# Order of the block products in a seven-product projection, the short convolution of the second strip in halves, and the place of one load wait

## The chip, the cores and the metric

The kernel runs on one core of one Trainium2 chip. The metric is the device time of one execution in microseconds (us), lower is better. Three runs of the kernel before gave 2369.01, 2370.47 and 2370.71 us, median 2370.47 us. All data are float32.

## What is computed

One hybrid decoder layer on 1024 tokens of width 1024. The change touches the input projection and what stands directly behind it:

```
y    = rmsnorm(x, norm_mix_g)
proj = y @ w_in                      # columns: u 512, v 512, q|k|v 1536, z 512, a 4, b 4
u, v, qkv, z, a, bb = split(proj)
out_a = gmlp_chunk_mixer(gelu(u), rmsnorm(gelu(v), gm_norm_g), gm_ws, gm_bs)
qkv  = silu(causal_dwconv(qkv, conv_w))          # 4 taps over the tokens, per channel
q, k = l2norm(q), l2norm(k)                      # per head of 128 channels
out_b = rmsnorm(gated_delta_rule(q, k, v, g, beta), dn_norm_g) * silu(z)
h    = x + concat(out_a, out_b) @ w_out
h    = h + moe_ffn(rmsnorm(h))       # top 4 of 32 experts, clamped SwiGLU
out  = rmsnorm(h, final_norm_g)
```

The factors `dn_norm_g` of the output norm are folded into silu(z) here.

## The kernel before

The program is three blocks with a barrier of all engines between them: projections, mixers (gMLP gate, delta rule, output projection, router) and the expert FFN. The change lies in the first block. Every engine runs its own list in program order and meets the others only at semaphores; DMAs are issued by SyncE in the order of its list.

**First half of the block: tokens by tiles (t = 0 to 7, 128 tokens each).** For tile t + 1 ScalarE sums the squares of x (`x_square`), VectorE scales them to a mean, GpSimd takes the inverse root (`x_root`, which calls `rsqrt`, L225), VectorE scales x (L583), TensorE transposes it (L456), VectorE writes it to `yT` with the norm's gain (L589). TensorE multiplies tile t with the u, v, z, a and b columns of `w_in` in four pieces n = 0 to 3 of 384 or 392 columns (L491); the transposes of tile t + 1 stand between pieces 1 and 2. At t = 0 piece 2 also waits until VectorE has copied the transposed parameters (L572 to L574, semaphore `par_done`), and that copy stands behind `x_out(1)` in VectorE's list. GpSimd normalises v (L300, L303) and multiplies silu(z) of the tile before with `dn_norm_g` (`z_gain`, L289). Ahead of this loop GpSimd waits for two loads, `gmg_in` (L254) and `dng_in` (L259):

```
x_root(0)
pool.wait_ge(S("gmg_in"), 16)
pool.wait_ge(S("dng_in"), 16)
for t in range(TT):
    if t + 1 < TT:
        x_root(t + 1)
```

**Second half: q, k and v by strips (u = 0 to 5, 256 channels each).** The output is kept transposed, channels on partitions, tokens along the free axis. A strip has a first chunk (c = 2u) and a second one (c = 2u + 1) of 128 channels, and each has a `lo` and a `hi` half of 512 tokens. The four quarters come from seven block products p = 0 to 6 instead of eight (`product`, 4 steps of 128 x 512 each, L504), with sums of weight blocks (`sA`, GpSimd, `weight_sums`) and of columns (`tB`, VectorE). Product n of all 42 goes to PSUM bank n mod 6. VectorE adds the products up (`combine`, L673, in place in `cb[0]` and `cb[1]`), runs the four taps (`conv`, L654 and L657), and ScalarE applies silu (L389, L393). For the eight chunks of q and k ScalarE then squares (L400), TensorE sums over the channels (`square_sums`, L514), ScalarE takes the inverse root and VectorE scales (`normalise`, L666). The second chunk is convolved in one piece of 1024 tokens, after the sixth product; the first chunk in two halves.

After the last strip GpSimd sets the state to zero (L334) once all silus are done, VectorE makes the decay factors (L706, L707), and all engines meet (L710 to L714). The next block begins for TensorE at L949.

## Time and profile before

| what | value |
|---|---|
| median of three runs | 2370.47 us |
| the profiled execution: time, span | 2367.14 us, 2365.4 us (1.74 us lie outside the span) |
| mean granted TensorE clock | 0.983 |
| TensorE matmuls busy | 2279.1 us, 96% |
| VectorE, GpSimd, ScalarE busy | 754.2 us (32%), 586.8 us (25%), 371.2 us (16%) |
| token tiles (L491), first matmul to the last strip's start | 11.87 to about 206 us |
| strips (L504, L514) | 206.29 to 366.59 us |
| next block's first matmul | 375.86 us |

TensorE is busy nearly everywhere, so what counts is where it stands still or runs at a lower clock. A timeline row gives the start, the time from the first to the last instruction of a merged run (in us), the engine, the line, the operands and the count; in brackets stands the idle time of that engine ahead of it and what ended it. SPq is SyncE's issue of a DMA. PEld is TensorE loading weights, beside its matmuls.

### The profile page before, as it was taken

How to read it: one execution, taken by the hardware profiler on the slowest of the kernel's cores; microseconds unless marked ns; L12 is line 12 of the kernel's file. 1: busy time of each engine (PE TensorE's matmuls, PEld its weight loads, DVE VectorE, ACT ScalarE, POOL GpSimd, SP SyncE). 2: the span in 40 equal slices, each digit the busy share in tenths (PEclk: the TensorE clock that was granted, in tenths of full speed). 3: DMA queues.
4: the chain of work that ended last, by engine and by line, in shares of the span. 5: the costliest groups of instructions: out<-in, count | busy, mean ns of one | idle time of the engine just before them, and what ended most of it. 6: DMA issues, size and time to landing. Idle time of an engine off the chain costs nothing.

```text
span 2365.4 us, 36376 instructions
## 1 busy us (share of the span) xinstructions
PE 2279.1 (96%) x14407; PEld 1918.6 (81%) x14408; DVE 754.2 (32%) x1722; ACT 371.2 (16%) x832; POOL 586.8 (25%) x809
## 2 busy tenths in 40 slices
PE   6999997999994999999999999999999999999996
PEld 4665446788774999999999999998887887878875
DVE  2133776454542135122222222222221221222223
ACT  1222553233221100011111111110000000000002
POOL 0213112222422122222222222232222222222212
PEclk9999998999996999999999999999999999999998
DMA  7000103011015866667788888889999999999995
GB/s 256 1 0 16 38 18 130 18 37 54 28 37 194 277 203 215 224 232 242 251 256 267 256 290 283 292 283 315 334 322 330 332 324 336 322 325 336 328 325 211
DMA packets 374770, 504.98 MB, mean 213 GB/s; under 512 B 12503, under 2 KB 288411, under 8 KB 374552
## 3 DMA queue, kind: packets, MB, share of 16 engines
q1 hardware_dynamic: 359704, 458.50, 57.7%
q0 software_dynamic: 14896, 44.14, 7.1%
q8 instruction: 116, 1.90, 0.3%
q14 instruction: 54, 0.44, 0.1%
HBM read 471.12 MB, written 34.13 MB: 214 GB/s over the span
## 4 chain that ended last, share of the span: by engine, by line
PE 67%; DMA 1%; DVE 0%; issue 0%; POOL 0%; ACT 0%; DVEq 0%; ACTq 0%; POOLq 0%
PE ps L1621 43%; PE ps L1648 11%; PE ps L1633 9%; PE ps L1600 2%; PE ps L1609 1%; DMA arena<-h_dram,arena 1%; DMA arena<-list_dram 0%; DVE arena L1832 0%; POOL arena L1463 0%; POOL small L225 0%; DVE arena L1859 0%; DVE arena L1866 0%; DVE arena L1875 0%; DVEq L1869 0%; ACT arena L1537 0%
## 5 line engine op out<-in xcount | busy, mean ns | idle before, releaser
L1621 PEld LDWEIGHTS ps<-arena 128*128 128x128 f32 x8192 | 1031.1, 191 | 9.3 <-issue 7.7
L1621 PE MATMUL ps<-arena 128*128 128x128 f32 (+15 forms) x8192 | 1037.6, 288 | 0.8 <-DVE arena L1766 0.8
L1790 DVE TENSOR_SCALAR arena<-ps,arena 128x128 f32<-128x128 f32 (+15 forms) x256 | 94.6, 370 | 1111.8 <-PE ps L1621 1108.3
L1460 POOL TENSOR_TENSOR arena<-arena 128x128 f32<-128x128 f32 (+15 forms) x256 | 132.3, 517 | 874.1 <-DVEq L1797 874.1
L1532 ACT ACTIVATE arena<-arena 128x128 f32<-128x128 f32 (+15 forms) x256 | 83.3, 325 | 1219.6 <-DVE arena L1790 1219.6
L1648 PE MATMUL ps<-arena 128*128 128x224 f32 (+14 forms) x1920 | 272.4, 303 | 0.0
L1648 PEld LDWEIGHTS ps<-arena 128*128 128x128 f32 x1920 | 270.1, 189 | 0.2
L1633 PE MATMUL ps<-arena 128*128 128x512 f32 x544 | 236.3, 592 | 0.0
L1633 PEld LDWEIGHTS ps<-arena 128*128 128x128 f32 x544 | 102.0, 190 | 122.0 <-issue 121.5
L491 PE MATMUL ps<-arena 128*128 128x384 f32 (+1 forms) x512 | 173.4, 498 | 3.1 <-DVEq L575 2.3
L491 PEld LDWEIGHTS ps<-arena 128*128 128x128 f32 x512 | 98.3, 195 | 70.7 <-issue 4.2
L504 PE MATMUL ps<-arena 128*128 128x512 f32 x336 | 146.3, 593 | 0.8 <-DVE arena L629 0.8
L1463 POOL TENSOR_TENSOR arena<-arena 128x128 f32<-128x128 f32 (+15 forms) x256 | 127.2, 497 | 20.1
L504 PEld LDWEIGHTS ps<-arena 128*128 128x128 f32 x336 | 63.6, 190 | 80.4 <-issue 78.4
L939 PE MATMUL ps<-arena 128*128 128x128 f32 x896 | 117.6, 283 | 4.8 <-DVE arena L1192 2.9
L225 POOL TENSOR_TENSOR small<-small,cst 128x4 f32<-128x4 f32 (+1 forms) x35 | 27.7, 795 | 358.4 <-DVE small L222 335.4
L939 PEld LDWEIGHTS ps<-arena 128*128 128x128 f32 x896 | 109.9, 195 | 6.8 <-issue 3.6
L1099 PE MATMUL ps<-arena 128*128 128x512 f32 x256 | 113.0, 595 | 0.8 <-DVE arena L1235 0.8
L1099 PEld LDWEIGHTS ps<-arena 128*128 128x128 f32 x256 | 47.5, 190 | 56.0 <-issue 54.5
L1791 DVE TENSOR_SCALAR arena<-ps,arena 128x128 f32<-128x128 f32 (+15 forms) x256 | 92.4, 361 | 0.0
L1438 POOL DMA_INDIRECT arena<-h_dram,arena x47 | 47.1, 1002 | 173.1 <-DMA arena<-list_dram 155.6
L1552 ACT ACTIVATE arena<-ps,arena 128x224 f32<-128x224 f32 (+14 forms) x120 | 48.0, 400 | 242.4 <-PE ps L1648 242.4
(253 smaller groups left out, 1583.5 us busy)
## 6 DMA issues: line engine op xcount, KB each, us to landing
arena<-in_exp_w_gu SPq DMA_DIRECT2D x256, 1024.0 KB, 7.8
arena<-in_exp_w_down SPq DMA_DIRECT2D x64, 2048.0 KB, 9.1
arena<-in_exp_b_down SPq DMA_DIRECT2D x17, 512.0 KB, 10.9
arena<-in_x SPq DMA_DIRECT2D x16, 512.0 KB, 9.5
arena<-in_w_in SPq DMA_DIRECT2D x8, 1024.0 KB, 7.2
h_dram<-arena SPq DMA_DIRECT2D x16, 512.0 KB, 2.6
arena<-in_w_out SPq DMA_DIRECT2D x1, 4096.0 KB, 12.8
arena<-h_dram SPq DMA_DIRECT2D x8, 512.0 KB, 7.0
```

Of the source, the lines that this page charges most:

```text
L491: last = t_.matmul(bank(bk)[:, to:to + width], yT[:, k, t * P:(t + 1) * P], wuvz[:, k, c0:c0 + width], start=(k == 0), stop=(k == KT - 1))
L504: last = t_.matmul(to, left[:, k, :], right[:, k, :], start=(k == 0), stop=(k == KH - 1))
L939: last = t_.matmul(out_bank[:, c], left[:, c], right[:, c], start=start, stop=stop)
L1099: last = t_.matmul(bank(4 * s + 1 + n), mixT[s][:, k, :], wout[:, k, 512 * n:512 * (n + 1)], start=(k == 0), stop=(k == KT - 1))
L1460: v.tensor_tensor(gmn[m % 2][:, 0:n], gmn[m % 2][:, 0:n], umn[m % 2][:, 0:n], ALU.mult).then_inc(S("gum", m % 2), 1)
L1463: v.tensor_tensor(hT[:, m, 0:n], gmn[m % 2][:, 0:n], sg[m % 2][:, 0:n], ALU.mult).then_inc(S("hT"), 1)
L1532: a.activation(sg[m % 2][:, 0:n], gmn[m % 2][:, 0:n], ACT.Sigmoid, scale=ALPHA).then_inc(S("sg", m % 2), 1)
L1621: last = t_.matmul(bank(m % 4)[:, q * CAP:q * CAP + n], wslot[g][:, k, 256 * q + c:256 * q + c + P], xT[:, k, 0:n], start=(k == 0), stop=( ...
L1633: last = t_.matmul(bank(6 + q), hT[:, k, 0:P], wslot[4 + q][:, k, :], start=(k == 0), stop=(k == KT - 1))
L1648: last = t_.matmul(bank(6 + d % 2)[:, 0:n], wslot[g][:, k, c:c + P], hT[:, k, 0:n], start=(k == 0), stop=(k == KT - 1))
L1790: v.tensor_scalar(gmn[r][:, 0:n], bank(m % 4)[:, 0:n], of[:, m:m + 1], LIMIT, ALU.add, ALU.min).then_inc(S("gmn", r), 1)
L1791: v.tensor_scalar(umn[r][:, 0:n], bank(m % 4)[:, CAP:CAP + n], of[:, 8 + m:9 + m], LIMIT, ALU.add, ALU.min)
```

## The change

- The products at places 4 and 5 are exchanged: w22 with `tB[2]`, which completes the second chunk's `lo` half, now comes at place 4, and `sA[0]` with `tB[0]` at place 5. The storage places of `sA[0]` and `sA[1]` are exchanged, and GpSimd's sums of the next strip wait for one product more.
- The second chunk is convolved in two halves: `lo` behind product 4, `hi` behind product 5. Its silu is in halves too. The waits on counts follow.
- GpSimd's wait for `dng_in` moves from ahead of the tile loop into the pass t = 4. The eight `z_gain` are done two at a time at t = 4 to 7, and so the last one comes ahead of `weight_sums(0)`.
- The decay factors stand before the last product is added in the last strip, and ScalarE makes their exponentials after the silu of the second chunk's `lo` half.
- The state is set to zero after product 42, not after the last silu.

```diff
-        sA = [r3(cut(512, big0 + 1024 * 11), KH), r3(cut(512, big0 + 1024 * 11 + 512), KH), r3(cut(512, big0 + 1024 * 10 + 512), KH)]
+        sA = [r3(cut(512, big0 + 1024 * 11 + 512), KH), r3(cut(512, big0 + 1024 * 11), KH), r3(cut(512, big0 + 1024 * 10 + 512), KH)]
...
             x_root(0)
             pool.wait_ge(S("gmg_in"), 16)
-            pool.wait_ge(S("dng_in"), 16)
...
                 v.tensor_tensor(vn, vsq, gmg[:], ALU.mult).then_inc(S("vn"), 1)
-                if t:
-                    z_gain(t - 1)
+                if t == 4:
+                    pool.wait_ge(S("dng_in"), 16)
+                if t >= 4:
+                    z_gain(2 * t - 8)
+                    z_gain(2 * t - 7)
...
                 if u:
-                    pool.wait_ge(S("prod"), 7 * u - 2)
+                    pool.wait_ge(S("prod"), 7 * u - 1)
...
             weight_sums(0)
-            z_gain(TT - 1)
...
-            pool.wait_ge(S("silu", 0), 12)
-            pool.wait_ge(S("silu", 1), 6)
+            pool.wait_ge(S("prod"), 42)
             v.memset(Sm, 0.0).then_inc(S("state_zero"), 1)
...
-            def silu_half(u, hf):
-                act.wait_ge(S("cacc", 0), 2 * u + hf + 1)
+            def silu_half(c, hf):
+                s, u = c % 2, c // 2
+                act.wait_ge(S("cacc", s), 2 * u + hf + 1)
                 half = slice(512 * hf, 512 * (hf + 1))
-                a.activation(qkvT[:, 2 * u, half], cacc[0][:, half], ACT.Silu).then_inc(S("silu", 0), 1)
-
-            def silu_second(u):
-                act.wait_ge(S("cacc", 1), u + 1)
-                a.activation(qkvT[:, 2 * u + 1, :], cacc[1], ACT.Silu).then_inc(S("silu", 1), 1)
+                a.activation(qkvT[:, c, half], cacc[s][:, half], ACT.Silu).then_inc(S("silu", s), 1)
...
-                    act.wait_ge(S("cacc", 1), u)
+                    act.wait_ge(S("cacc", 1), 2 * u)
...
-                    silu_second(u - 1)
+                    silu_half(2 * u - 1, 1)
                     if u <= 4:
                         squares(2 * u - 1)
-                    silu_half(u - 1, 1)
+                    silu_half(2 * u - 2, 1)
...
-                silu_half(u, 0)
+                silu_half(2 * u, 0)
                 if 1 <= u <= 4:
                     norm_roots(2 * u - 1)
                     norm_roots(2 * u - 2)
                 if u == 5:
+                    act.wait_ge(S("sum"), 24)
+                silu_half(2 * u + 1, 0)
+                if u == 5:
                     act.wait_ge(S("gc_ready"), 1)
...
-            act.wait_ge(S("sum"), 24)
-            silu_second(5)
-            silu_half(5, 1)
+            silu_half(11, 1)
+            silu_half(10, 1)
...
                 if u:
-                    pe.wait_ge(S("p_add"), 7 * u - 1)
+                    pe.wait_ge(S("p_add"), 7 * u - 3)
...
                 product(u, 3, w_part(u, 0, 1), y_part(0, 1))
-                product(u, 4, sA[0], tB[0])
+                if u:
+                    pe.wait_ge(S("p_add"), 7 * u - 1)
+                product(u, 4, w_part(u, 1, 1), tB[2])
...
-                product(u, 5, w_part(u, 1, 1), tB[2])
+                product(u, 5, sA[0], tB[0])
...
+            def decay_factors():
+                dve.wait_ge(S("ga_egc"), 1)
+                v.scalar_tensor_tensor(sub_all[:], sub_all[:], -1.0, be_all[:], ALU.mult, ALU.mult)
+                v.tensor_tensor(bx_all[:], bx_all[:], be_all[:], ALU.mult).then_inc(S("gates_done"), 1)
...
                 dve.drain()
-                combine(u, 4, first[:, hi], first[:, hi])
+                combine(u, 4, second[:, lo], second[:, hi], ALU.subtract)
+                if u:
+                    dve.wait_ge(S("silu", 1), 2 * u)
+                conv(2 * u + 1, 0, 512)
+                combine(u, 5, first[:, hi], first[:, hi])
+                combine(u, 5, second[:, hi], second[:, hi])
+                conv(2 * u + 1, 512, 512)
                 if 1 <= u <= 4:
                     normalise(2 * u - 1)
-                combine(u, 5, second[:, lo], second[:, hi], ALU.subtract)
-                combine(u, 4, second[:, hi], second[:, hi])
-                if u:
-                    dve.wait_ge(S("silu", 1), u)
-                conv(2 * u + 1, 0, SEQ)
+                if u == 5:
+                    decay_factors()
                 combine(u, 6, first[:, hi], first[:, hi])
...
-            dve.wait_ge(S("ga_egc"), 1)
-            v.scalar_tensor_tensor(sub_all[:], sub_all[:], -1.0, be_all[:], ALU.mult, ALU.mult)
-            v.tensor_tensor(bx_all[:], bx_all[:], be_all[:], ALU.mult).then_inc(S("gates_done"), 1)
```

The order of GpSimd's first instructions, before: its first inverse root (tile 0), the second one (tile 1), and the v norm of tile 0. In brackets stand the semaphores that an instruction waits for.

```order
L225 TENSOR_TENSOR small<-small,cst 128x1 [waits x_var,cst_in]
L225 TENSOR_TENSOR small<-small,cst 128x1 [waits x_var,dng_in,gmg_in]
L225 TENSOR_TENSOR small<-small,cst 128x4 [waits v_var]
L300 TENSOR_TENSOR arena<-arena,small 128x512 [waits v_rs]
L303 TENSOR_TENSOR arena<-arena,gmg 128x512 [waits vn_free,vn_a]
```

The same place in the changed kernel:

```order
L225 TENSOR_TENSOR small<-small,cst 128x1 [waits x_var,cst_in]
L225 TENSOR_TENSOR small<-small,cst 128x1 [waits x_var,gmg_in]
L225 TENSOR_TENSOR small<-small,cst 128x4 [waits v_var]
L299 TENSOR_TENSOR arena<-arena,small 128x512 [waits v_rs]
L302 TENSOR_TENSOR arena<-arena,gmg 128x512 [waits vn_free,vn_a]
```

The inverse root of tile 1 no longer waits for `dng_in`; everything behind it in GpSimd's list moves with it.

VectorE's list in the last strip (u = 5), before, from the additions of products 2 and 3 to its end. L673 adds a product, L654 and L657 are the four taps, L706 and L707 the decay factors.

```order
L673 TENSOR_TENSOR arena<-arena,ps 128x512 [waits prod] x2
L689 COPY gc_all<-ps 128x32 [waits gc_ps]
L673 TENSOR_TENSOR arena<-arena,ps 128x512 [waits prod] x3
L654 TENSOR_SCALAR arena<-arena,vT 128x1024 [waits silu_1]
L657 SCALAR_TENSOR_TENSOR arena<-arena,vT 128x1024 x3
L673 TENSOR_TENSOR arena<-arena,ps 128x512 [waits prod]
L654 TENSOR_SCALAR arena<-arena,vT 128x512 [waits silu_0]
L657 SCALAR_TENSOR_TENSOR arena<-arena,vT 128x512 x3
L706 SCALAR_TENSOR_TENSOR sub_all<-sub_all,be_all 128x32 [waits ga_egc]
L707 TENSOR_TENSOR bx_all<-bx_all,be_all 128x32
```

In the changed kernel, from the addition of product 4 (L679 adds, L660 and L663 are the taps, L653 and L654 the decay factors):

```order
L679 TENSOR_TENSOR arena<-arena,ps 128x512 [waits prod]
L660 TENSOR_SCALAR arena<-arena,vT 128x512 [waits silu_1]
L663 SCALAR_TENSOR_TENSOR arena<-arena,vT 128x512 x3
L679 TENSOR_TENSOR arena<-arena,ps 128x512 [waits prod] x2
L660 TENSOR_SCALAR arena<-arena,vT 128x512
L663 SCALAR_TENSOR_TENSOR arena<-arena,vT 128x512 x3
L653 SCALAR_TENSOR_TENSOR sub_all<-sub_all,be_all 128x32 [waits ga_egc]
L654 TENSOR_TENSOR bx_all<-bx_all,be_all 128x32
L679 TENSOR_TENSOR arena<-arena,ps 128x512 [waits prod]
L660 TENSOR_SCALAR arena<-arena,vT 128x512 [waits silu_0]
L663 SCALAR_TENSOR_TENSOR arena<-arena,vT 128x512 x3
```

The taps of 1024 tokens behind three additions have become two of 512, the first behind one addition and the second behind two more, and the decay factors have moved ahead of the last addition.

## Rows read from the trace of the kernel before

**Rows 1.** Waits of TensorE, whole run: line waited at, releaser; total, times, longest.

```profile
PE ps L949 <- PEq L714: 9.3, 1, 9.3
```

**Rows 2.** Timeline of TensorE, tiles 0, 1 and 4: start, us, what, idle before.

```profile
21.34 5.33 PE L491 MATMUL ps<-arena 128*128 128x384 f32 x16
...
32.72 1.97 PE L456 MATMUL ps<-cst,arena 128*128 128x128 f32 x8 [6.05 <-DVE arena L583]
37.03 12.69 PE L491 MATMUL ps<-arena 128*128 128x384 f32 x32 [2.34 <-DVEq L575]
...
61.64 10.59 PE L491 MATMUL ps<-arena 128*128 128x384 f32 x32
...
128.31 1.04 PE L456 MATMUL ps<-cst,arena 128*128 128x128 f32 x8
```

**Rows 3.** Timeline of GpSimd and VectorE, tile 0; the last row tile 4.

```profile
31.32 0.55 POOL L225 TENSOR_TENSOR small<-small,cst 128x1 f32<-128x1 f32 x1 [23.05 <-DMA dng<-in_dn_norm_g]
31.91 0.75 DVE L583 TENSOR_SCALAR arena<-arena,small 128x1024 f32<-128x1024 f32 x1 [12.64 <-POOL small L225]
...
34.73 0.69 DVE L589 TENSOR_TENSOR arena<-ps,vT 128x512 f32<-128x512 f32 x1 [0.16 <-PE ps L456]
...
36.27 0.68 DVE L574 TENSOR_TENSOR wsT<-ps,cst 128x512 f32<-128x512 f32 x1
...
128.95 1.29 DVE L589 TENSOR_TENSOR arena<-ps,vT 128x512 f32<-128x512 f32 x2 [7.32 <-PE ps L456]
```

**Rows 4.** Timeline of SyncE's DMA issues, first 20 us.

```profile
14.18 0.69 SPq L254 DMA_DIRECT2D gmg<-in_gm_norm_g  x1
...
18.41 2.17 SPq L257 DMA_DIRECT2D arena<-in_w_in  x1
```

**Rows 5.** DMA issues, first 70 us: size, us from issue to landing.

```profile
arena<-in_w_in SPq DMA_DIRECT2D x1, 1568.0 KB, 11.3
...
gmg<-in_gm_norm_g SPq DMA_DIRECT2D x1, 256.0 KB, 6.7
```

**Rows 6.** Windows: us, PE, PEld, DVE, ACT, POOL busy (x), PEclk, DMA share, GB/s.

```profile
30.00:31.00 1.00, 0.00 (x0) 0.00 (x0) 0.00 (x0) 0.00 (x0) 0.00 (x0) 0.92 1.03 410
...
368.00:370.00 2.00, 0.00 (x0) 0.00 (x0) 1.93 (x3) 0.51 (x1) 0.00 (x0) 0.69 0.00 0
```

**Rows 7.** Timeline of all engines, end of the last strip and next block's start.

```profile
359.76 0.69 DVE L673 TENSOR_TENSOR arena<-arena,ps 128x512 f32<-128x512 f32 x1 [2.64 <-PE ps L504]
...
363.20 1.29 DVE L673 TENSOR_TENSOR arena<-arena,ps 128x512 f32<-128x512 f32 x2 [2.75 <-PE ps L504]
...
365.40 4.00 DVE L657 SCALAR_TENSOR_TENSOR arena<-arena,vT 128x1024 f32<-128x1024 f32 x3
...
370.67 2.40 DVE L657 SCALAR_TENSOR_TENSOR arena<-arena,vT 128x512 f32<-128x512 f32 x3
...
373.09 0.18 DVE L707 TENSOR_TENSOR bx_all<-bx_all,be_all 128x32 f32<-128x32 f32 x1
373.10 0.63 ACT L389 ACTIVATE arena<-arena 128x512 f32<-128x512 f32 x1 [1.26 <-DVE arena L657]
373.79 0.52 POOL L334 MEMSET arena<- 128x512 f32 x1 [30.04 <-ACT arena L389]
...
375.86 0.66 PE L949 MATMUL ps<-cst,gc_all 128*128 128x128 f32 x2 [9.27 <-PEq L714]
```

**Rows 8.** Timeline of all engines, strips 0 and 1.

```profile
225.02 4.21 DVE L657 SCALAR_TENSOR_TENSOR arena<-arena,vT 128x512 f32<-128x512 f32 x3
...
228.65 1.72 POOL L315 TENSOR_TENSOR arena<-arena 128x512 f32<-128x512 f32 x1
...
234.50 4.00 DVE L657 SCALAR_TENSOR_TENSOR arena<-arena,vT 128x1024 f32<-128x1024 f32 x3
...
240.23 1.06 ACT L400 ACTIVATE arena<-arena 128x1024 f32<-128x1024 f32 x1
...
242.18 0.19 PEld L514 LDWEIGHTS ps<-arena,cst 128*128 128x128 f32 x1 [0.24 <-issue]
```

**Rows 9.** Windows, strip 1 from its first `square_sums` to strip 2's.

```profile
242.60:270.10 27.50, 27.50 (x66) 12.19 (x65) 20.52 (x26) 17.45 (x21) 5.81 (x4) 1.00 0.13 38
```

## The prediction

> **What bounds the kernel now.** I read the page first: TensorE's matmuls are busy 96% of the span, so only the places where TensorE stands still or runs slowly are open to a change. The list of its waits says where. In the stretch that the edits touch it has two places of weight: 9.3 us at the barrier behind the last strip [rows 1], and, in the timeline of tile 0, 6.05 us ahead of the transposes of tile 1 and 2.34 us behind them [rows 2]. Between 61 and 366 us the strips and tiles run almost without a gap, so what VectorE, ScalarE and GpSimd do there is covered, as long as it stays covered.
>
> **Start: the wait for the output norm's factors.** The reader is to follow the 6.05 us backwards. The transposes waited for VectorE's scaling of tile 1 at 31.91, this for GpSimd's inverse root at 31.32, and this, after 23.05 us of idling, for the DMA of the factors [rows 3]. The inverse root itself does not need them; it merely stands behind the wait in the queue. TensorE had nothing to do from 26.67 (21.34 + 5.33) on [rows 2].
>
> After the change the same instruction waits for the v norm's factors alone. They were issued at 14.18 and landed 6.7 us later, at 20.9 [rows 4, 5]. The root then runs from 21.0 to 21.6 (0.55, with the 0.1 that the row before shows between landing and start), the scaling ends at about 22.4 (0.75) [rows 3]. That is before 26.67, so the transposes of tile 1 no longer wait at all.
>
> What is late next? Piece 2 of tile 0 waits for VectorE's copy of the parameters, which stands behind the two writes of tile 1 to `yT`. Transposes from 26.5 to 27.6 (1.04 us where they run without a gap before them) [rows 2]; the pair of writes begins 0.64 after the transposes (128.95 against 128.31) and takes 1.29 [rows 2, 3], so it ends at 28.4; the copies took 1.53, from 35.42 (34.73 + 0.69) to 36.95 (36.27 + 0.68) [rows 3], so they end at 30.0. TensorE goes on at 30.0 instead of 37.03 [rows 2]: **7.0 us**. The third weight piece (1568 KB) was issued at 18.41 and landed at 29.7 [rows 4, 5]; piece 3 wants it only some 5 us after 30.0, so it stays covered.
>
> On top comes the clock. The 32 matmuls behind the gap took 12.69 us, the same 32 of tile 1 took 10.59 [rows 2]: 2.1 us lost at the lower granted level (0.50, which is 1.2 GHz, against 2.4). The clock fell late within 30 to 31, 4.1 us after the last matmul [rows 6]; at the end of the strips it fell at about 368.8 (a mean of 0.69 over two us means 1.24 us at 0.50), only 2.2 us after TensorE's last matmul at 366.6 [rows 6, 7]. A gap of 2.5 us (27.6 to 30.0) is left in tile 0. It lies between 2.2 and 4.1, nearer to the shorter. I take it that the clock falls there again and that the 2.1 us stay lost; if it does not, the gain at the start is 9.1. So the start gives 7.0, bounds 6.3 (a longer low stretch than before) and 9.1.
>
> Moving the eight gain multiplications costs GpSimd time only: before, they ran one a tile, now two in each of the last four. The last one now waits for the last silu(z) and stands ahead of the weight sums of strip 0, which come some 2 us later than before. Product 2 is the first to use them, behind two products and a gate, so this is covered; uncovered it would be at most these 2 us. I take 0.
>
> **End: the tail behind the last product.** TensorE ends at 366.6 and resumes at 375.86 [rows 7]. The chain between is VectorE's: pair of additions from 363.20, taps of 1024 tokens to 369.40 (365.40 + 4.00), the last addition and taps of 512 to 373.07 (370.67 + 2.40), the last silu from 373.10 to 373.73, GpSimd's zeroing of the state from 373.79 to 374.31, and 1.55 us of barrier [rows 7]. Addition plus taps of 512 cost 3.67 (373.07 less 369.40), the taps alone 3.0 (less 0.68).
>
> After the change: addition of product 4 at 359.76, as before, since it is still the fifth product; the taps of `lo` end at 363.5 (359.76 + 0.69 + 3.0). Product 5 is there at about 363.2, so the pair of additions runs to 364.8 and the taps of `hi` to 367.8. Two factor instructions of 0.18, started 0.1 apart [rows 7], make 0.2; the last addition then starts at about 368.0 and its taps end at 371.7 (3.67 more). ScalarE's exponentials are due between, but `lo` is done at 363.5, 4 us earlier. Silu to 372.4. The zeroing now runs behind the last product, beside the taps; it may delay them by up to half its 0.52. So ScalarE arrives at 372.4 to 372.7, against 374.31: 1.6 to 1.9 us, of which 0.58 come from the zeroing and the rest from the halved taps. I take **1.7 us**.
>
> **Middle: strips 0 to 4.** Halving the taps adds one instruction start to each: 3.0 + 3.0 instead of 4.8 without company, 1.2 us a strip, VectorE work that TensorE does not wait for. In a strip of 27.50 us VectorE was busy 20.52 [rows 9]. GpSimd's sums now run one product (3.4 us) later, beside the taps of the second chunk instead of beside `normalise`. What their company costs: three taps of 512 took 4.21 us, against 2.40 alone, while GpSimd's sums ran to 230.37 [rows 7, 8]. The tightest place is `square_sums(1)` in strip 1: the squares it needs were done at 241.29 (240.23 + 1.06) and TensorE wanted them at 242.18 [rows 8], 0.9 us of slack. Before, the taps of chunk 1 ended at 238.50. After: the taps of chunk 0 `lo` run without company and end 1.8 us earlier, at 227.4; three additions to 229.6 (0.69 each); taps of `lo` with about 2.3 us of company to 234.9; the pair 1.3; taps of `hi` 3.0; end 239.3. That is 0.8 later, and the last silu is the half one (0.63 for 1.06), so the squares are done at about 241.7, 0.5 before TensorE wants them. Bounds: no wait, or 1.3 us if the company costs 1.8 more. I take 0.1. From strip 1 on, with q the end of product 5: pair and taps of `hi` with company end at q + 6.3, copy, silu and squares at about q + 10.5 (0.6 + 0.63 + 1.06 and what lies between), and TensorE wants them four products later, at q + 13.8: 3 us of slack.
>
> By the Trainium skill, SBUF — State Buffer, section "SBUF: two separate sides", VectorE instructions with two SBUF inputs and GpSimd instructions that read SBUF take a port pair as an exclusive lock, and the loser blocks for the whole instruction. The trace agrees only in part: 1.81 us were lost in at most 4.21 us of company [rows 8], less than half. By the rule in full, the taps of chunk 1 would stand for all of GpSimd's four sums; that is the second rival below.
>
> **Sum.** 7.0 + 1.7 - 0.1 = 8.6 us. The profiled execution took 2367.14 (span 2365.4 and 1.74 around it), so it becomes 2358.5. The median of the runs shown is 3.3 us above it, and the difference carries over: 2370.47 - 8.6 = **2361.9 us**. The blocks behind start earlier as a whole; nothing in them waits for something older than the barrier.
>
> **The rivals.**
> 1. *The clock holds.* Gap of 2.5 us too short: gain 9.1 + 1.7 - 0.1 = 10.7, 2359.8 us. For it: at tile 0 the clock held 4.1 us [rows 6]. Against: only 2.2 us at the tail.
> 2. *The company of GpSimd and VectorE is a full lock.* Overlap of the `lo` taps with the sums then costs up to 4.1 instead of 2.3, the squares come at 243.5, TensorE stands 1.3 us in strip 1; the later strips have 3 us and hold. Gain 7.3, 2363.2 us. Against it is the lower price in [rows 8].
> 3. *The start does not give its 7.0.* Another load or VectorE's copies keep piece 2 until about 35. Then the gain is 2 to 4 us, 2367.5 us. Against it: the landing times [rows 4, 5].
> 4. *Slower: VectorE becomes the bound of the strips.* Place: `square_sums` and the additions ahead of bank reuse in strips 1 to 4. Its work a strip is 20.52 + 1.2 + the company; it decides from 27.5 us a strip on, 5.8 us more than I count [rows 9]. To end 5 us slower the four strips must each lose 3.4 us, VectorE 30.9 us a strip: 2375.5 us.
>
> **How the numbers follow.** Forecast 0.50, rival 1 0.28, rival 2 0.10, rival 3 0.10, rival 4 0.02. The forecast's own range is 2360.5 to 2363.5. The range of 2358 to 2365 holds it, rivals 1 and 2, and the scatter of the median (the three runs lie within 1.7 us), and leaves out rivals 3 and 4 and a little at both ends. A measurement of this kernel can tell about 0.2%, 4.7 us, from no change, so faster means under 2365.7: forecast, rivals 1 and 2 and a part of rival 3, 0.90; same 0.08; slower 0.02.
>
> **What would show it.** In the timeline after: the inverse root of tile 1 at about 21.0 behind the v norm's factors; transposes at 26.5 without a wait; piece 2 at 30.0; the granted clock between 28 and 34 decides between forecast and rival 1. At the end a gap of 7.5 us instead of 9.27 with ScalarE's silu as the last work in it. No row of TensorE waiting at `square_sums` over 0.5 us; one of 1 us or more speaks for rival 2. A piece 2 later than 32 makes the prediction wrong at its largest term.

## The result and the profile after

The changed kernel takes 2357.03 us (median of 5 runs, 2356.53 to 2359.07); the kernel before took 2370.47 beside it (5 runs, 2369.01 to 2371.12). The ratio is 0.9947, with a 95% interval of 0.9934 to 0.9961. Measured again later it was 2357.69 against 2369.47, 0.9953 (0.9940 to 0.9967). So the kernel became 13.4 us faster, where the forecast said 8.6; the time lies 1 us below the range of 2358 to 2365. Between the two profiled executions the difference is smaller: 2367.14 and 2356.53, 10.6 us.

The waits of TensorE in the changed kernel, in the form of [rows 1] (line waited at, releaser; total, times, longest):

```profile
PE ps L956 <- PEq L721: 7.0, 1, 7.0
...
PE ps L490 <- DVEq L576: 2.5, 1, 2.5
PE ps L455 <- DVE arena L584: 2.5, 1, 2.5
```

L956 is the barrier behind the last strip: 7.0 us instead of 9.3. L490 is piece 2 of tile 0, which waits for VectorE's copies of the parameters as foretold. The wait at L455 lies ahead of the transposes of tile 0, at the very start; before, that line waited twice, 8.5 us in total, and the longer of the two, the 6.05 us of [rows 2], is gone.

TensorE's timeline in tile 0 of the changed kernel (start, us, what, idle before), to be held against [rows 2]:

```profile
20.88 5.33 PE L490 MATMUL ps<-arena 128*128 128x384 f32 x16
26.05 1.04 PE L455 MATMUL ps<-cst,arena 128*128 128x128 f32 x8
29.58 10.69 PE L490 MATMUL ps<-arena 128*128 128x384 f32 x32 [2.50 <-DVEq L576]
40.11 1.05 PE L462 MATMUL ps<-arena,wsT 128*128 128x128 f32 x8
```

The transposes of tile 1 follow piece 1 without a wait. Piece 2 begins at 29.58 instead of 37.03, and its 32 matmuls take 10.69 us, not 12.69: they ran at the full level of the clock. The last row, the first gate of tile 0, serves below as a mark. Before, its row was this one:

```profile
49.55 1.05 PE L463 MATMUL ps<-arena,wsT 128*128 128x128 f32 x8
```

GpSimd and VectorE there, as in [rows 3]:

```profile
19.91 0.56 POOL L225 TENSOR_TENSOR small<-small,cst 128x1 f32<-128x1 f32 x1 [11.80 <-DMA gmg<-in_gm_norm_g]
20.50 0.75 DVE L584 TENSOR_SCALAR arena<-arena,small 128x1024 f32<-128x1024 f32 x1 [2.22 <-POOL small L225]
...
26.68 1.29 DVE L590 TENSOR_TENSOR arena<-ps,vT 128x512 f32<-128x512 f32 x2 [5.42 <-PE ps L455]
...
28.82 0.68 DVE L575 TENSOR_TENSOR wsT<-ps,cst 128x512 f32<-128x512 f32 x1
```

The root waits for the v norm's factors, no longer for the output norm's, and starts at 19.91 instead of 31.32. VectorE now idles for TensorE's transposes (5.42 us) and not the other way round.

The end of the last strip, all engines, as in [rows 7]:

```profile
353.98 1.28 DVE L679 TENSOR_TENSOR arena<-arena,ps 128x512 f32<-128x512 f32 x2
...
355.92 2.40 DVE L663 SCALAR_TENSOR_TENSOR arena<-arena,vT 128x512 f32<-128x512 f32 x3
357.21 0.52 POOL L334 MEMSET arena<- 128x512 f32 x1 [21.38 <-PE ps L503]
...
359.78 2.40 DVE L663 SCALAR_TENSOR_TENSOR arena<-arena,vT 128x512 f32<-128x512 f32 x3
362.21 0.63 ACT L390 ACTIVATE arena<-arena 128x512 f32<-128x512 f32 x1 [3.23 <-DVE arena L663]
364.11 1.09 PE L956 MATMUL ps<-cst,gc_all 128*128 128x128 f32 x4 [6.96 <-PEq L721]
```

TensorE ends the last product at 357.15 (364.11 less 6.96). The zeroing of the state runs in its shadow at 357.21 and does not slow the taps beside it: three taps take 2.40 us as they do alone. The last silu ends at 362.84, and no GpSimd work follows it. TensorE's gap is 6.96 us instead of 9.27.

Four marks carry the accounting (us from the start of the span): the first gate, the end of the last product, the start of the next block, and the first gather by token, where a DMA ends a long stretch of small matmuls. "Before, again" is a second profile of the kernel before, from the experiments.

| | first gate | last product ends | next block | gather | span |
|---|---|---|---|---|---|
| before | 49.55 | 366.59 | 375.86 | 746.24 | 2365.4 |
| before, again | 48.93 | 365.97 | 375.23 | 751.41 | 2368.8 |
| after | 40.11 | 357.15 | 364.11 | 735.02 | 2354.8 |
| after, again | 40.15 | 357.19 | 364.16 | 734.93 | 2355.0 |

Gate to last product is 317.04 us in all four. Against the first profile of before, the gate comes 9.44 sooner and the tail is 2.31 shorter, together 11.75, of which 10.6 are left at the end: 0.5 are lost between the barrier and the gather and 0.6 behind the gather. Against the second, gate and tail make 11.1, 5.3 more come out of the block between barrier and gather, in which the change moves nothing, and 14.0 are left at the end, so 2.4 are lost behind the gather.

### The profile page after: what moved, and what is told of

Same layout as the page of the kernel before. It is cut to its first block, busy times and chain, and to the rows that moved or that the text cites. A ratio compares the mean times of both kernels' runs of the same rounds, so it can differ in the third digit from the quotient of the medians.

```text
span 2354.8 us, 36430 instructions
## 1 busy us (share of the span) xinstructions
PE 2277.3 (97%) x14407; PEld 1918.6 (81%) x14408; DVE 759.3 (32%) x1746; ACT 371.7 (16%) x838; POOL 588.2 (25%) x809
## 4 chain that ended last, share of the span: by engine, by line
PE 67%; DMA 1%; DVE 0%; issue 0%; POOL 0%; ACT 0%; DVEq 0%; ACTq 0%; POOLq 0%
PE ps L1628 43%; PE ps L1655 11%; PE ps L1640 9%; PE ps L1607 2%; PE ps L1616 1%; DMA arena<-h_dram,arena 1%; DMA arena<-list_dram 0%; DVE arena L1839 0%; POOL arena L1470 0%; POOL small L225 0%; DVE arena L1866 0%; DVE arena L1873 0%; DVE arena L1882 0%; DVEq L1876 0%; ACT arena L1544 0%
## 5 line engine op out<-in xcount | busy, mean ns | idle before, releaser
L490 PE MATMUL ps<-arena 128*128 128x384 f32 (+1 forms) x512 | 171.6, 494 | 3.3 <-DVEq L576 2.5
L490 PEld LDWEIGHTS ps<-arena 128*128 128x128 f32 x512 | 97.4, 193 | 69.7 <-DVEq L576 2.7
## 6 DMA issues: line engine op xcount, KB each, us to landing
arena<-in_exp_b_down SPq DMA_DIRECT2D x17, 512.0 KB, 10.6
```

Source lines behind the costliest of these rows:

```text
L490: last = t_.matmul(bank(bk)[:, to:to + width], yT[:, k, t * P:(t + 1) * P], wuvz[:, k, c0:c0 + width], start=(k == 0), stop=(k == KT - 1))
```

## The experiments

**The wait alone.** The kernel before, with only the wait moved. It stands behind the v norm of tile 1, since nothing here multiplies gains in the later tiles alone.

```diff
-            pool.wait_ge(S("dng_in"), 16)
 ...
+                if t == 1:
+                    pool.wait_ge(S("dng_in"), 16)
```

> The kernel before with the wait for dng_in alone moved behind the v norm of tile 1; strips and tail as before. Theory A (the start carries the gain, the granted clock holds over the 2.5 us gap that is left in tile 0): TensorE takes up piece 2 of tile 0 at about 29.6 us instead of 37.0 and reaches the first gate at 40.1 instead of 49.55, 9.4 us earlier; span 9 to 10 us shorter, median about 2361. Theory B (the clock falls in that gap, as forecast): 7.0 to 7.4 us, median about 2363.3, with the granted clock at 0.50 after 30 us. Both: a gap of 9.3 us at the barrier as before.

Measured: 2362.21 us (10 runs), ratio 0.9972 (0.9962 to 0.9981). TensorE in tile 0:

```profile
20.10 5.33 PE L492 MATMUL ps<-arena 128*128 128x384 f32 x16
...
28.80 12.29 PE L492 MATMUL ps<-arena 128*128 128x384 f32 x32 [2.50 <-DVEq L576]
...
40.93 1.05 PE L464 MATMUL ps<-arena,wsT 128*128 128x128 f32 x8
```

The wait brings its seven microseconds by itself, and 7.4 between the medians. The gap of 2.50 is the same as in the changed kernel, but here the clock fell in it: 32 matmuls take 12.29 us instead of 10.69. So neither the forecast nor rival 1 is right as a rule about a gap of 2.5 us.

**The strips alone.** The changed kernel, with the wait back ahead of the loop.

```diff
+            pool.wait_ge(S("dng_in"), 16)
 ...
-                if t == 4:
-                    pool.wait_ge(S("dng_in"), 16)
```

> The changed kernel with the wait for dng_in back ahead of the tile loop; halves, exchanged products and tail as changed. Theory A: TensorE resumes at 37.0 in tile 0 as before and the gap at the barrier is 7.0 us, so 2.3 us less than before, median about 2368.2. Rival (the strips gain or lose something of their own beyond the tail): the time from the first strip to its last product differs from the 160.3 us of before by over 0.5 us.

Measured: 2365.32 us (11 runs), ratio 0.9983 (0.9974 to 0.9992). Its waits of TensorE have the short gap at the barrier, and its timeline the late start of the transposes:

```profile
PE ps L955 <- PEq L720: 7.0, 1, 7.0
...
31.33 1.97 PE L454 MATMUL ps<-cst,arena 128*128 128x128 f32 x8 [5.10 <-DVE arena L583]
```

By the pooled median of before (2369.57, 26 runs) this is 4.3 us faster, by the ratio 4.0 (1.9 to 6.2). The gap accounts for 2.3, which is what was expected; the time from the first gate to the last product is 317.03 us, so the strips give nothing of their own. No run here assigns the other 2 us; the interval of this run just holds 2.3. The two halves together make 7.4 + 4.3 = 11.7 of the 13.4. What is left, 1.7, is as large as the clock's 1.6 in tile 0, but it is also within the scatter of the medians, and no run tells the two apart.

**Before again.** The kernel before, unchanged, to see how far executions of one kernel differ.

> The kernel before, unchanged, once more with its own profile. If the 3.3 us between the first profiled execution and the medians is scatter of the granted clock from run to run, the spans of its executions differ by 1 to 4 us, a longer span comes with a lower mean clock, and the profile shows where: stretches at 0.50 that the first profile did not have, or longer ones behind the same gaps. If instead the first profile was a usual run and the difference is systematic, all executions lie within 0.5 us of each other. Ratio to the kernel before: 1.000.

Measured: 2369.83 us (11 runs), ratio 1.0003 (0.9994 to 1.0012). All 26 runs of the kernel before beside it lie between 2365.0 and 2371.6 us, and the profiled one took 2370.48. So the first profile, 2367.14, was of one of the faster executions. The block between barrier and gather shows why (windows: us; PE, PEld, DVE, ACT, POOL busy with counts; PEclk; DMA share; GB/s). Before:

```profile
375.86:724.75 348.89, 330.56 (x2112) 263.89 (x2113) 178.11 (x391) 100.05 (x273) 103.08 (x94) 0.97 0.15 56
```

Before again:

```profile
375.23:729.56 354.33, 334.34 (x2112) 268.09 (x2112) 178.11 (x391) 100.05 (x273) 103.05 (x94) 0.96 0.15 55
```

After:

```profile
364.11:713.39 349.28, 331.18 (x2112) 264.90 (x2112) 178.17 (x391) 99.95 (x273) 103.14 (x94) 0.97 0.15 56
```

The same 2112 matmuls take 348.89 or 354.33 us. VectorE, ScalarE and GpSimd are equally busy; TensorE is busy 3.8 us longer, and its mean granted clock is lower. From the barrier to the gather the profiles of the kernels here took between 370.4 and 376.2 us. Behind the gather two levels are seen as well: 1617.4 us here and 1617.3 in one profile below (a gap of 4), 1619.2 to 1620.4 in the eleven others.

**Parameters first.** The changed kernel, with VectorE's copy of the parameters ahead of the writes of tile 1, so that no gap is left ahead of piece 2.

```diff
                     x_scale(t + 1)
-                    x_out(t + 1)
                 if t == 0:
                     parameters()
+                if t + 1 < TT:
+                    x_out(t + 1)
```

> The changed kernel with VectorE's copy of the parameters ahead of the two writes of tile 1 to yT. Theory A: the 2.5 us gap ahead of piece 2 of tile 0 goes, since the copies fall under piece 1; TensorE goes straight on at about 27.1 and the span is 2.4 us shorter than that of the changed kernel, median about 2354.5. Rival (something else holds piece 2, such as its weights, landed at about 25 to 30): a gap stays, at another releaser, and less than 1 us is gained.

Measured: 2355.86 us (5 runs, 2354.44 to 2356.91), ratio 0.9945 (0.9931 to 0.9958).

```profile
25.53 1.04 PE L455 MATMUL ps<-cst,arena 128*128 128x128 f32 x8
26.40 10.59 PE L490 MATMUL ps<-arena 128*128 128x384 f32 x32
```

The gap is gone, and the first gate comes at 36.83, 3.3 before that of the changed kernel. But at the gather the profile stands at 735.17 against 735.02: the block between took 3.4 us more. The median gains 1.2, where 2.5 had been expected. What is won at the start arrives at the barrier whole; what arrives at the end depends also on the clock in the block behind.

**The zeroing late again.** The changed kernel, with the state zeroed only behind the last silu.

```diff
-            pool.wait_ge(S("prod"), 42)
+            pool.wait_ge(S("silu", 0), 12)
+            pool.wait_ge(S("silu", 1), 12)
```

> The changed kernel with the zeroing of the state waiting for all silus again. If the tail ends with ScalarE's silu and the barrier takes 1.5 us more whoever arrives last, the gap at the barrier is 7.0 + 0.6 = 7.6 us (0.06 to the start of the zeroing and 0.52 for it). If GpSimd's arrival is cheaper than ScalarE's, it is less than 7.5.

Measured: 2360.94 us (one run).

```profile
PE ps L957 <- PEq L722: 7.8, 1, 7.8
...
363.75 0.52 POOL L335 MEMSET arena<- 128x512 f32 x1 [27.07 <-ACT arena L391]
365.81 0.45 PE L957 MATMUL ps<-cst,gc_all 128*128 128x128 f32 x1 [7.82 <-PEq L722]
```

The gap grows from 6.96 to 7.82 us, more than the 0.58 of the zeroing. From the last engine's end to TensorE's restart it is 1.54 us where GpSimd comes last (364.27 to 365.81) and 1.27 where ScalarE does (362.84 to 364.11). This is nearly half of what my tail term missed. The time is 3.9 us above the changed kernel's median, but the tail explains only 0.9 of it; the first gate came 0.8 later (40.95), because the clock fell in tile 0, and the block behind the barrier took 373.6 us instead of 370.9. Of a single run, then, the rows can be compared and the time can't.

**The taps in one piece.** The changed kernel, with the second chunk's 1024 tokens convolved at once. In the last strip ScalarE also makes the exponentials ahead of that chunk's silu.

```diff
 ...
-                conv(2 * u + 1, 0, 512)
 ...
-                conv(2 * u + 1, 512, 512)
+                conv(2 * u + 1, 0, SEQ, 2)
```

> The changed kernel with the taps of the second chunk in one piece of 1024 tokens behind the additions of products 4 and 5 (and the exponentials ahead of that chunk's silu). If the halves are what shortens VectorE's tail, the last taps end 1.2 to 1.7 us later and the gap at the barrier is 8.4 to 8.9 us against 7.0; if it is only the exchanged products, it stays near 7.0. The time from the first gate to the last product stays 317.0 us in both.

Measured: 2360.88 us (one run).

```profile
PE ps L954 <- PEq L719: 8.7, 1, 8.7
...
356.59 4.00 DVE L662 SCALAR_TENSOR_TENSOR arena<-arena,vT 128x1024 f32<-128x1024 f32 x3
```

A gap of 8.68 us, as expected: the halved taps are worth 1.72 and the early zeroing 0.86 of the tail, each undone by itself; together they are worth 2.31. The sum of the two is 0.27 too much: with the taps in one piece VectorE ends 6.74 us behind the last product, 0.26 later than in the kernel before, since the decay factors now stand ahead of the last addition. Gate to last product is 317.04 here too, so halving the taps costs TensorE nothing in the strips.

**A gap of 4.** The changed kernel, with the last copy of the parameters done three times; it writes the same values again.

```diff
-                v.tensor_tensor(wsT[:], heads(bank(6)), over_heads(tri), ALU.mult)
-                dve.drain()
+                for _ in range(3):
+                    v.tensor_tensor(wsT[:], heads(bank(6)), over_heads(tri), ALU.mult)
+                    dve.drain()
```

> The changed kernel with the last parameter copy of VectorE done three times, so that TensorE's gap ahead of piece 2 of tile 0 is about 4.0 us instead of 2.5. If the length of the gap decides, the granted clock is at 0.50 behind it (it fell 4.1 and 2.2 us after TensorE's last matmul in the first profile) and the 32 matmuls take over 12 us. If it holds here as in the changed kernel, they take 10.7. Span longer by 1.5 us, or by 3 to 4 where the clock falls.

Measured: 2357.04 us (one run). The gap of TensorE is 4.0 us, the clock fell, and from the restart at 30.97 to the gate at 43.11 it is 12.14 us, against 10.53 in the changed kernel. The gate comes 3.0 us later than the changed kernel's, yet the time is the same, where 1.5 or 3 to 4 us more had been expected: the next block begins 3.4 us later, the gather comes 2.95 later, and behind the gather 2.4 us come back.

```profile
PE ps L490 <- DVEq L577: 4.0, 1, 4.0
```

**Strip 0 late.** The changed kernel, with two additions of 512 put into VectorE's queue ahead of the second half's taps in strip 0; they write into a buffer that nothing reads any more.

```diff
+                if u == 0:
+                    dve.drain()
+                    for _ in range(2):
+                        dve.drain()
+                        v.tensor_tensor(usq[0][:, 0, :], second[:, lo], second[:, hi], ALU.add)
```

> The changed kernel with two more additions of 512 on VectorE (1.5 us) ahead of the taps of chunk 1 hi in strip 0 alone. The changed kernel's squares(1) end at 232.90 and TensorE's weights for square_sums(1) are due at 232.74, so the cover is just gone: TensorE should stand 1.3 to 1.6 us ahead of square_sums(1), and the time from the first gate to the last product should be 318.3 to 318.6 us against 317.04. If my count of the slack (0.5 us) were right, it would be 318.0; if the later strips or something else give cover, 317.0.

Measured: 2359.49 us (one run).

```profile
235.87 1.99 PE L513 MATMUL ps<-arena,cst 128*128 128x512 f32 x4 [1.21 <-ACT arena L397]
```

TensorE now waits 1.2 us for the squares in strip 1, and gate to last product is 318.51, 1.47 longer than in every other kernel here, as expected. An addition takes 0.69. So strip 1 has no slack left: what VectorE does there in addition goes to TensorE nearly in full.

**After again.** The changed kernel, unchanged.

> The changed kernel, unchanged, once more. The rows that do not depend on luck (TensorE's restart in tile 0, 7.1 us earlier on the mean, one to two and a half us less at the lower clock behind it, 2.3 us less at the barrier) add up to 10.3 us, and 11.9 where the clock holds in tile 0. If the 13.4 us of the first comparison held 1.5 to 3 us of luck with the clock in the second block, the median is now about 2358.5 to 2359 against a median before of 2369.6, ratio 0.9955. If it is systematic, the median stays at 2357.0, ratio 0.9947. In its profile the clock falls in the 2.5 us gap, as it did in four of the five profiles that have this gap.

Measured: 2357.69 us (5 runs), ratio 0.9953 (0.9940 to 0.9967).

```profile
20.93 5.33 PE L490 MATMUL ps<-arena 128*128 128x384 f32 x16
...
29.62 10.69 PE L490 MATMUL ps<-arena 128*128 128x384 f32 x32 [2.50 <-DVEq L576]
```

I had expected the clock to fall this time, and it held again. That is not yet the rule for this schedule. Three of the runs above, the zeroing late again, the taps in one piece and strip 0 late, are the changed kernel in everything that any engine does in tile 0; their edits act 180 us later or more. In all three the clock fell. They ran on another chip than this one; the wait alone ran on this one's, and there the clock fell too. The rows are piece 0 of the changed kernel, then pieces 0 and 2 with the zeroing late again, then pieces 0 and 2 with strip 0 late:

```profile
11.71 8.25 PE L490 MATMUL ps<-arena 128*128 128x384 f32 x16 [0.79 <-DVE arena L590]
...
11.85 6.97 PE L491 MATMUL ps<-arena 128*128 128x384 f32 x16 [0.78 <-DVE arena L591]
...
28.85 12.27 PE L491 MATMUL ps<-arena 128*128 128x384 f32 x32 [2.50 <-DVEq L577]
...
11.54 8.05 PE L490 MATMUL ps<-arena 128*128 128x384 f32 x16 [0.78 <-DVE arena L590]
...
29.21 12.39 PE L490 MATMUL ps<-arena 128*128 128x384 f32 x32 [2.50 <-DVEq L576]
```

So for one and the same tile 0 the clock held in two profiles and fell in three. The first row is from the first profile of the changed kernel; in the second one piece 0 took 8.36 us.

**Two early.** As with the parameters first, and also VectorE's copy of the factor vectors (`vT`) behind the scaling of tile 0, which needs none of them.

```diff
-            dve.wait_ge(S("vec_T"), 1)
-            v.tensor_copy(vT[:], ps[:, 3, 0:NV])
-            dve.drain()
 ...
             x_scale(0)
+            dve.wait_ge(S("vec_T"), 1)
+            v.tensor_copy(vT[:], ps[:, 3, 0:NV])
+            dve.drain()
 ...
```

> Parameters first, as in e4, and also VectorE's copy of the norm's factors behind the scaling of tile 0 instead of ahead of it. The copy then runs while TensorE transposes tile 0: the first transposes start 0.7 us earlier (8.2 instead of 8.96), and all behind them. No gap ahead of piece 2. Against the changed kernel 3.3 us (no gap and no low clock) and 0.7: median 2354 to 2355. If the first weights (landed near 11 us) are what piece 0 waits for, the 0.7 is not seen in TensorE's restart at 11.7.

Measured: 2351.27 us (5 runs, 2349.75 to 2355.55), ratio 0.9928 (0.9915 to 0.9942). It beats both kernels, the changed one by 5.8 us between the medians and by 3.4 between the profiled executions.

```profile
8.26 1.97 PE L455 MATMUL ps<-cst,arena 128*128 128x128 f32 x8 [1.80 <-DVE arena L577]
11.01 8.45 PE L490 MATMUL ps<-arena 128*128 128x384 f32 x16 [0.78 <-DVE arena L583]
...
26.43 10.59 PE L490 MATMUL ps<-arena 128*128 128x384 f32 x32
```

The first transposes start at 8.26 instead of 8.96. Yet piece 2 starts at 26.43 and the gate at 36.85, no sooner than with the parameters first alone. The 0.7 is lost in piece 0, whose 16 matmuls begin that much sooner and take 8.45 us instead of 7.77. What differs in the profiles lies behind the barrier: the gather comes at 731.64 against 735.17. So the 0.7 of the `vT` edit gave nothing by itself in these rows. Between 370 and 700 us its trace has the granted clock at 0.50 from 375.6 to 379.0 and from 645.2 to 648.6; with the parameters first it is at 0.50 from 374.8 to 381.7, from 480.6 to 484.1 and from 647.9 to 651.3, so about 7 us longer, which fits the 3.5. The median is 4.6 better than with the parameters first. Whether the `vT` edit brings that lastingly, by way of the clock, or whether it is scatter, no run shows.

**The gap moved.** The changed kernel with the `vT` edit alone; the gap of 2.5 us stays, but all of it comes sooner.

```diff
-            dve.wait_ge(S("vec_T"), 1)
-            v.tensor_copy(vT[:], ps[:, 3, 0:NV])
-            dve.drain()
 ...
             x_scale(0)
+            dve.wait_ge(S("vec_T"), 1)
+            v.tensor_copy(vT[:], ps[:, 3, 0:NV])
+            dve.drain()
 ...
```

> The changed kernel with VectorE's copy of the norm's factors behind the scaling of tile 0, and the parameter copies where the changed kernel has them: the gap of 2.5 us ahead of piece 2 of tile 0 stays as long, and everything from tile 0 on begins about 0.6 us earlier. In the profiles so far the clock held where piece 1 began at 20.88 or 20.93 and fell where it began at 19.79 to 20.51. If the place of the gap decides, piece 1 begins near 20.4 here and the clock falls: the 32 matmuls behind the gap take 12.2 to 12.5 us. If the changed kernel holds its clock for another reason, they take 10.7.

Measured: 2358.51 us (one run).

```profile
19.96 5.33 PE L490 MATMUL ps<-arena 128*128 128x384 f32 x16
...
28.66 12.38 PE L490 MATMUL ps<-arena 128*128 128x384 f32 x32 [2.50 <-DVEq L569]
```

The same piece 1, the same transposes, the same gap of 2.50, begun 0.9 us sooner, and the clock fell. The gate comes at 40.88, later than the changed kernel's 40.11 although everything ahead of it is earlier. The outcome is the one expected of the place in time, but the run does not test it: piece 1 began at 19.96 and not near 20.4, because piece 0 took 7.41 us (8.25 in the changed kernel), and with the clock rising that early it fell in tile 0 without any move as well.

## Why the prediction was right in kind and wrong in size

**The start's 7.0.** Right. In the seven profiles with a gap of 2.5 us, piece 2 restarts at 28.49 to 29.62, in the mean at 29.03, against 36.06 in the three with the old wait: 7.0 us. For the pair of profiles that the sum was made from it is 7.45 (37.03 to 29.58). The steps on the way are there: root behind the v norm's factors, transposes without a wait, piece 2 waiting for VectorE's copies.

**"I take it that the clock falls there again ... and that the 2.1 us stay lost."** This is the step that failed within the kernel; a second one, "the difference carries over", follows below. The windows of the changed kernel (columns as above, PEclk before the DMA share) show the full level on both sides of the restart:

```profile
29.00:30.00 1.00, 0.42 (x1) 0.30 (x2) 0.88 (x2) 0.00 (x0) 0.00 (x0) 1.00 1.04 397
30.00:31.00 1.00, 1.00 (x5) 0.59 (x4) 0.47 (x2) 0.00 (x0) 0.37 (x1) 1.00 1.02 406
```

With the wait alone moved, they do not:

```profile
28.00:29.00 1.00, 0.20 (x1) 0.20 (x2) 0.88 (x3) 0.00 (x0) 0.00 (x0) 0.82 1.00 386
29.00:30.00 1.00, 1.00 (x2) 0.63 (x3) 0.69 (x2) 0.00 (x0) 0.15 (x1) 0.50 1.07 400
```

In [rows 6] I had set two lengths of idling against each other, 2.2 and 4.1 us, and taken the nearer. The runs show that the length alone does not decide. At one length, 2.50 us, after the same 16 matmuls and 8 transposes, the clock held where piece 1 had begun at 20.88 and 20.93, and fell to 0.50 where it had begun at 19.79, 19.96, 20.10, 20.15 and 20.51. Where it holds, 10.5 us lie between restart and gate; where it falls, 12.1 to 12.2; in the three profiles with the old wait, 12.5 to 13.4 (mean 13.1). Even the fall is thus cheaper than before, by 0.9 in the mean, a gain that the forecast had at 0. Nor does the schedule decide: in five of the seven profiles tile 0 is the same program, and there it held twice and fell three times.

What differs from one execution to the next is the clock ahead of the gap. The same 16 matmuls of piece 0 took 8.25 and 8.36 us where the clock later held, 8.05 with strip 0 late, and 6.97 to 7.41 in the other four. By the trace's record of the clock it had risen in piece 0 at 17.4 and 17.6 us, at 16.9, and at 14.8 to 15.1. Where it had risen at 14.8 to 15.1 it fell at 28.4 to 28.7, inside the gap; where it had risen at 16.9 it fell only at 30.5, 1.3 us behind the restart, as this window of strip 0 late shows:

```profile
30.00:31.00 1.00, 1.00 (x4) 0.64 (x3) 0.17 (x1) 0.00 (x0) 0.73 (x1) 0.75 1.04 414
```

When piece 1 begins follows from how long piece 0 takes, so its place in time and the moment at which the clock rose fit the seven profiles equally well, and no run here separates them. Which of the two outcomes an execution gets was in any case luck as far as this kernel's code goes, and the profiled pair had the good one. The Trainium skill, TensorE: Matmul & The Clock Gate, section "Part 1: The HAM clock gate", says that the gate judges activity on a rhythm of its own that "doesn't reset when your kernel starts". By the first half of that, a gap of one length can go either way, as here. By the second half one kernel should go either way from execution to execution, and the traces agree: held twice, fallen three times with one and the same tile 0. For the pair of profiles that the sum was made from, rival 1 gave 10.7 us and 10.6 were measured.

**The tail's 1.7.** The mechanism is right, the size is not: 2.31 (9.27 to 6.96). VectorE's last taps end 5.03 us behind the last product (357.15 to 362.18), not 6.48 (366.59 to 373.07), which is 1.45; the zeroing gives 0.58, and 0.27 comes from the barrier, which is cheaper when ScalarE arrives last. I had put VectorE's end at 371.7, 5.1 behind the product, and so had this right; what I missed was the barrier's 0.27, and I had set aside up to 0.3 for a zeroing that would slow the taps, which it does not.

**Middle, 0.1.** Right in outcome: 317.04 us from gate to last product in before and after alike. In detail my margin of 0.5 us at strip 1 is used up. VectorE's timeline of the changed kernel in strip 0:

```profile
220.23 1.06 DVE L660 TENSOR_SCALAR arena<-arena,vT 128x512 f32<-128x512 f32 x1
221.72 4.58 DVE L663 SCALAR_TENSOR_TENSOR arena<-arena,vT 128x512 f32<-128x512 f32 x3 [0.43 <-issue]
```

and GpSimd's beside it:

```profile
219.74 1.26 POOL L314 TENSOR_TENSOR arena<-arena 128x512 f32<-128x512 f32 x1 [15.17 <-PE ps L503]
...
224.04 1.71 POOL L321 TENSOR_TENSOR arena<-arena 128x512 f32<-128x512 f32 x1
```

The four taps take 6.07 us (220.23 to 226.30) instead of 3.0: 3.1 lost in 5.5 us of company, between my 2.3 and rival 2's 4.1. The squares then end just when TensorE wants them:

```profile
231.84 1.06 ACT L397 ACTIVATE arena<-arena 128x1024 f32<-128x1024 f32 x1
232.95 0.40 PEld L513 LDWEIGHTS ps<-arena,cst 128*128 128x128 f32 x2 [0.46 <-ACT arena L397]
233.16 1.88 PE L513 MATMUL ps<-arena,cst 128*128 128x512 f32 x4
```

The weight load waited 0.46 us, the matmuls not visibly. By the exclusive lock of the Trainium skill (SBUF — State Buffer, section "SBUF: two separate sides") the taps could have lost up to all 5.5; the measured loss is 56% of that. VectorE is busy 21.91 us of strip 1's 27.47, where it was 20.52 of 27.50 [rows 9]: 1.4 more, where I had counted 1.2 and rival 4 needed 5.8 on top of these.

```profile
233.16:260.63 27.47, 27.47 (x66) 12.16 (x64) 21.91 (x30) 17.47 (x22) 6.15 (x4) 1.00 0.13 38
```

**"The difference carries over."** It did not. The 3.3 us between the profiled time and the median of before came from one fast execution; both profiles of after, 2356.53 and 2356.77, lie within 1 us of their medians. The executions of the changed kernel scatter less (2356.5 to 2359.1 us) than those of before (2365.0 to 2371.6), so where a profile of before lies against its median does not say where that of after will lie, and the range should have held that doubt.

**What took the time out of the range.** The median gain is 13.44 us, 4.8 more than the 8.6 of the forecast. In the marks of the profiled pair this is made up of 0.45 at the restart, 2.0 of the clock, 0.6 at the tail and 0.1 in the middle, less 1.1 lost behind the barrier, and of 2.8 by which the difference between profile and median did not carry over (13.44 less 10.61). Neither the clock nor the 2.8 takes the time out of the range alone (rival 1 gives 2359.8); the two together do. Behind the 2.8 is the scatter of executions, which the forecast knew only as three runs within 1.7 us of each other.

**The account.** Mean gate of the three profiles with the old wait 49.16, after 40.11: 9.05. Tail 2.3. Together 11.4 us for the two profiled executions of the changed kernel: 6.5 are the earlier restart (36.06 to 29.58), 2.6 the clock (13.1 to 10.5 us from there to the gate), and 2.3 the barrier. Over all five profiles with the same tile 0 the mean gate is 40.66, 8.5 us earlier than before, and with the tail this gives 10.8; how often the clock holds in the other runs is not known. The medians say 13.4, the ratio 12.6 (9.2 to 15.6); in the second measurement 11.8. What lies above 11.4, if it is real, lies behind the barrier, in the block up to the gather or behind the gather, where the profiles differ by 5.8 and by 3 us. In the first of these the clock falls in different places in different profiles, of one kernel too. Whether this adds 1 or 2 us lastingly or is scatter stays open.

## What to carry to other kernels

A wait at the head of an in-order queue holds all that stands behind it, so follow a gap back until an instruction waits for something that it does not use; here one such line was worth 7.4 us between the medians by itself. When a sum is made against one profile, first see how far executions of that kernel scatter, and which block of it scatters. A short gap of TensorE can cost its length or its length and a fall of the clock; take both as ends of the range, and do not take the outcome of one or two profiles for the kernel's own. Where the gap can be closed by reordering two copies, close it; here that brought the gate 3.3 us forward and the median 1.2.

## What was not expected of the hardware

- The same gap of 2.50 us between the same matmuls leaves the clock at its full level or drops it to half (2.4 and 1.2 GHz), also in profiles of one and the same tile 0 (held twice, fell three times); 1.6 to 1.7 us lie between the two. The fall can come 1.3 us after the matmuls have gone on. With 4.04 us it fell, once.
- The barrier of all engines costs 1.27 us from ScalarE's end to TensorE's restart and 1.54 from GpSimd's.
- Four taps of 512 on VectorE lost 3.1 us in 5.5 us of company of GpSimd's two-input additions, and nothing beside GpSimd's zeroing.
- A block of 2112 small matmuls with an unchanged schedule takes 348.89 or 354.33 us.
